# Split query and key logits in a second attention, with earlier bias loads, respread row products and two softmax groups moved to GpSimd

## The reference, cut to what matters

```python
# first model, attention layer
logits = einsum('bqhc,bqkc->bqhk', q_lat, c_sel) + bias      # bias = rel_bias[t5_bucket(dist)]
p = softmax(logits)                                          # keys chosen by a top-k of a score
# adaLN of the second model
shift, scale, gate = split(silu(cond) @ w_ada + b_ada, 3)    # two rows cond: c and c_ctx
# second model, attention ("second attention" below): 8 heads of 64
q = rms_norm(heads(z_q), q_norm_g) * 64 ** -0.5
k = rms_norm(heads(z_k), k_norm_g)                           # latent keys and context keys
s = concat([q . k_local + rpb bias (or -1e30), q . k_context])
out = softmax(s) @ [v, v_context]
```

## Time and profile before

| what | value |
|---|---|
| median of 3 runs | 860.97 us (860.26 to 863.52) |
| profiled execution | 861.54 us, its span 859.5 us |
| TensorE busy | 848.9 us (99% of the span), granted clock 1.0 throughout |
| VectorE, ScalarE, GpSimd busy | 698.2, 484.3, 130.0 us |
| memory traffic | 167.88 MB, mean 195 GB/s |

### The profile page before, as it was taken

One profiled execution on the slowest core, in us unless ns is written; L12 is line 12 of the kernel. 1 busy time (PEld: TensorE's weight loads), 2 busy tenths in 40 slices (PEclk: granted clock), 3 DMA queues, 4 the chain that ended last, 5 costly groups with the idle time before them and its releaser, 6 DMA issues.

```text
span 859.5 us, 18107 instructions
## 1 busy us (share of the span) xinstructions
PE 848.9 (99%) x7062; PEld 813.6 (95%) x7062; DVE 698.2 (81%) x1096; ACT 484.3 (56%) x710; POOL 130.0 (15%) x147
## 2 busy tenths in 40 slices
PE   8999999999999999999999999999999999999998
PEld 7999999999999997799999999989899898999998
DVE  5998798898888899786667666677758998998895
ACT  6796555555444466765555444363367557645742
POOL 3140000014322000000000222132203314012000
PEclk9999999999999999999999999999999999999999
DMA  8744667779999730246666666576445554455552
GB/s 318 299 149 147 221 229 245 244 258 294 296 289 267 216 128 20 93 162 214 196 195 196 203 193 195 167 214 220 149 148 172 171 161 159 148 174 177 207 180 98
DMA packets 48050, 167.88 MB, mean 195 GB/s; under 512 B 5969, under 2 KB 7393, under 8 KB 47729
## 3 DMA queue, kind: packets, MB, share of 16 engines
q1 hardware_dynamic: 41840, 146.82, 52.0%
q0 software_dynamic: 5856, 20.00, 8.0%
q10 hardware_dynamic: 288, 0.15, 0.1%
HBM read 165.50 MB, written 1.44 MB: 194 GB/s over the span
## 4 chain that ended last, share of the span: by engine, by line
PE 74%; DVE 14%; DMA 6%; ACT 3%; issue 2%; SPq 0%; POOL 0%; DVEq 0%; ACTq 0%
PE bank L546 22%; PE bank L550 22%; PE bank L551 22%; DMA raw<-weights 5%; DVE wlo L1416 4%; DVE xc L1498 1%; DVE ada_prod L1558 1%; PE bank L813 1%; ACT whi L1030 1%; PE bank L898 1%; PE bank L900 1%; PE bank L899 1%; PE bank L939 1%; PE bank L949 1%; DMA x<-x_in 1%
## 5 line engine op out<-in xcount | busy, mean ns | idle before, releaser
L1416 DVE TENSOR_TENSOR wlo<-raw,whi 128x1024 fp32r<-128x1024 f32 x266 | 326.8, 1262 | 86.1 <-ACT whi L1030 85.5
L550 PE MATMUL bank<-xl,whi 128*128 128x256 f32 x1328 | 369.7, 278 | 0.0
L546 PE MATMUL bank<-xh,whi 128*128 128x256 f32 x1310 | 367.5, 281 | 1.9 <-DVE xl L1438 1.7
L551 PE MATMUL bank<-xh,wlo 128*128 128x256 f32 x1328 | 368.4, 277 | 0.0
L1030 ACT ACTIVATE whi<-raw 128x1024 fp32r<-128x1024 f32 x266 | 272.3, 1054 | 152.6 <-PE bank L551 99.6
L546 PEld LDWEIGHTS bank<-xh,whi 128*128 128x128 f32 x1310 | 245.8, 188 | 10.9 <-issue 7.1
L550 PEld LDWEIGHTS bank<-xl,whi 128*128 128x128 f32 x1328 | 249.4, 188 | 0.3
L551 PEld LDWEIGHTS bank<-xh,wlo 128*128 128x128 f32 x1328 | 249.2, 188 | 0.0
L551 PE MATMUL bank<-hhi,wlo 128*128 128x256 f32 x560 | 155.1, 277 | 0.0
L546 PE MATMUL bank<-hhi,whi 128*128 128x256 f32 x554 | 154.1, 278 | 0.0
L550 PE MATMUL bank<-hlo,whi 128*128 128x256 f32 x512 | 142.2, 278 | 0.0
(11 more groups left out here) (311 smaller groups left out, 1032.1 us busy)
## 6 DMA issues: line engine op xcount, KB each, us to landing
raw<-weights SPq DMA_DIRECT2D x266, 512.0 KB, 4.3
ada_raw<-ada_w POOLq DMA_DIRECT2D x24, 512.0 KB, 5.7
plain<-plain_w SPq DMA_DIRECT2D x8, 512.0 KB, 8.5
relB<-rel_scratch POOLq DMA_DIRECT2D x8, 256.0 KB, 8.8
bl<-rpb_in POOLq DMA_DIRECT2D x32, 64.0 KB, 3.4
plain<-plain_w SPq DMA_DIRECT2D x4, 256.0 KB, 5.7
cond<-cond_in POOLq DMA_DIRECT2D x1, 1024.0 KB, 8.5
cx<-ctx_in POOLq DMA_DIRECT2D x1, 1024.0 KB, 8.5
```

What stands on the lines that cost most here:

```text
L546: mmul(dst, hi, rh, start=start, stop=False)
L550: mmul(dst, hi, rlo, start=False, stop=False)
L551: return mmul(dst, lo, rh, start=False, stop=stop)
L1416: V_.tensor_tensor(wlo[:, sl], raw[:, sl], whi[:, sl].bitcast(F32), ALU.subtract)\
```

## The change

The logits of the second attention are made from split operands: ACT copies `kk` and `q2` into `hch` and `xh[8..11]` (`qk_hi`), DVE subtracts into `hcl` and `xl[8..11]` (`qk_lo`), and `logits2` makes three fp32r products for each head instead of one float32 product. Tile 0 of this is placed ahead of the split of the first chunks of cg on both engines, tiles 1 to 3 after the first unit of cg. The eight `relB` loads are issued right after the table is stored. The order of the adaLN rows is new: two gate rows are summed beside rec_out, eight rows beside up0, and the other fourteen over the tiles of down0 as listed in `ADA_DOWN`. The pieces of the first two plain chunks hold half a chunk's row each (2 KB). For the groups 0 and 1 of the first attention GpSimd scales the probabilities.

```diff
@@ -93,9 +93,10 @@
-ADA_ORDER = [0, 1, 2, 3, 4, 5, 6, 7, 8, 16, 9, 17, 10, 18, 11, 19, 12, 20, 13, 21, 14, 22, 15, 23]
+ADA_ORDER = [16, 17, 0, 1, 2, 3, 4, 5, 6, 7, 8, 18, 9, 19, 10, 20, 11, 21, 12, 13, 22, 14, 23, 15]
 ADA_M = 3 * DT
-ADA_DOWN = 8
+ADA_UP = 2
+ADA_DOWN = ((10, 11), (12, 13), (14, 15), (16, 17), (18,), (19, 20), (21, 22), (23,))
@@ -340,8 +341,8 @@
-                part = slice(j * CH // 4, (j + 1) * CH // 4)
-                sp.dma_start(plain[:, 0:2, part], plain_w[0:2, :, part].rearrange("c p n -> p c n")).then_inc(s_head[j], 16)
+                part = slice(j % 2 * CH // 2, (j % 2 + 1) * CH // 2)
+                sp.dma_start(plain[:, j // 2, part], plain_w[j // 2][:, part]).then_inc(s_head[j], 16)
@@ -427,6 +428,17 @@
+            def load_rel_bias(m):
+
+                p0 = m * RCOPY
+                pool.dma_start(relB[p0:p0 + RCOPY], bass.AP(tensor=rel_scratch.tensor, offset=P - 1 - p0,
+                                                            ap=[[H1 * RLEN - 1, RCOPY], [RLEN, H1], [1, S]]))\
+                    .then_inc(S_["rel_bias_loaded"], 16)
+
+            pool.wait_ge(S_["rel_stored"], 16)
+            for m in range(DT):
+                load_rel_bias(m)
+
             for h in range(2):
@@ -437,17 +449,10 @@
+            load_ada(2)
+            load_ada(3)
             pool.wait_ge(S_["chunk_used"], 2 * U0["up0"])
             pool.dma_start(cx[:], ctx_in).then_inc(S_["ctx_loaded"], 16)
-            for i in range(2, ADA_DOWN + 2):
-                load_ada(i)
-
-            def load_rel_bias(m):
-
-                p0 = m * RCOPY
-                pool.dma_start(relB[p0:p0 + RCOPY], bass.AP(tensor=rel_scratch.tensor, offset=P - 1 - p0,
-                                                            ap=[[H1 * RLEN - 1, RCOPY], [RLEN, H1], [1, S]]))\
-                    .then_inc(S_["rel_bias_loaded"], 16)
@@ -461,13 +466,13 @@
                 add_ctx_squares(m)
-                for i in (ADA_DOWN + 2 * m + 2, ADA_DOWN + 2 * m + 3):
-                    if i < ADA_M:
-                        load_ada(i)
-
+                for i in ADA_DOWN[m + 1] if m < DT - 1 else ():
+                    load_ada(i)
+
+            for m in range(DT):
+                load_ada(4 + m)
             pool.dma_start(wiw[:], wi_in).then_inc(S_["wi_loaded"], 16)
-            pool.wait_ge(S_["rel_stored"], 16)
-            squares_by_tile(3, 0, ahead_of_tile, load_rel_bias)
+            squares_by_tile(3, 0, ahead_of_tile)
@@ -477,6 +482,12 @@
                 G.tensor_tensor(cx[:, m], cx[:, m], rctx[:], ALU.mult).then_inc(S_["ctx_scaled"], 1)
+            for g in range(2):
+                pool.wait_ge(S_["sums_inverted"], g + 1)
+                for i in range(4):
+                    sl = slice(i * P, (i + 1) * P)
+                    ins = G.tensor_scalar(pt[:, g % 3, sl], pt[:, g % 3, sl], rden[:, g % 2, i:i + 1], None, ALU.mult)
+                ins.then_inc(S_["probs_ready"], 1)
             squares_by_tile(5, 1, scale_ctx)
@@ -621,10 +632,11 @@
                             pe.wait_ge(S_["xg_ready"], k + 1)
-                            mm = mmul(bank[2 * c][:, 0:S], plain[:, c, k * P:(k + 1) * P], gate[:, k],
+                            w0 = (4 * (j % 2) + 2 * c + k % 2) * P
+                            mm = mmul(bank[2 * c][:, 0:S], plain[:, j // 2, w0:w0 + P], gate[:, k],
                                       start=k == 0, stop=k == DT - 1)
-                        if j == 3:
-                            mm.then_inc(S_["plain_used"], 1)
+                    if j % 2:
+                        mm.then_inc(S_["plain_used"], 1)
@@ -930,14 +942,18 @@
                 t, b = p // 2, p % 2
-                if p == 0:
-                    pe.wait_ge(S_["qk_normed"], 8)
-                else:
+                if b == 0:
+                    pe.wait_ge(S_["qk_lo"], t + 1)
+                if p:
                     pe.wait_ge(S_["logits2_read"], 2 * p)
-                for e in range(2):
-                    lo = 64 * e
-                    mmul(LOGIT[e][:, :], q2[lo:lo + 64, t, b * P:(b + 1) * P], kk[lo:lo + 64, t], start=True, stop=True)\
-                        .then_inc(S_["logits2_full"], 1)
+                tok = slice(b * P, (b + 1) * P)
+                for n, (q, k) in enumerate(((xh, hch), (xh, hcl), (xl, hch))):
+                    for e in range(2):
+                        rows = slice(64 * e, 64 * e + 64)
+                        mm = mmul(LOGIT[e][:, :], q[rows, 8 + t, tok], k[rows, 2 * t:2 * t + 2].rearrange("p a n -> p (a n)"),
+                                  start=n == 0, stop=n == 2)
+                        if n == 2:
+                            mm.then_inc(S_["logits2_full"], 1)
@@ -1350,11 +1366,20 @@
             dsts = {"cg": (cg, ACT.Sigmoid), "za": (za, ACT.Silu), "cz": (cz, ACT.Silu), "bz": (bz, ACT.Silu)}
+            def qk_hi(t):
+                act.wait_ge(S_["qk_normed"], t + 1)
+                A(hch[:, 2 * t:2 * t + 2], two(kk[:, t]), ACT.Copy).then_inc(S_["qk_hi"], 1)
+                act.wait_ge(S_["qk_normed"], BT + t + 1)
+                A(xh[:, 8 + t], q2[:, t], ACT.Copy).then_inc(S_["qk_hi"], 1)
+            qk_hi(0)
             ahead(U0["ca"] + 1)
...
                     ahead(U0[name] + i)
+                    if name == "cg" and i == 0:
+                        for t in range(1, BT):
+                            qk_hi(t)
                     if name in dsts:
@@ -1553,7 +1578,7 @@
                         ch.wait()
-                    else:
+                    elif used is not None:
                         dve.wait_ge(S_["ada_used"], used)
@@ -1565,7 +1590,7 @@
                 dve.wait_ge(s_adaw[i % 2], 16 * (i // 2 + 1))
-                ada_sums(i % 2, i, lambda c: ada[:, t, c:c + 1], 1 if t >= 2 * DT else 2)
+                ada_sums(i % 2, i if i else None, lambda c: ada[:, t, c:c + 1], 1 if t >= 2 * DT else 2)
@@ -1620,19 +1645,18 @@
-                i0, c = (-5, -5, -4, -4)[r], r % 2
-                n = 2 * i0
+                i0, c = (-3, -3, -2, -2)[r], r % 2
+                n = 2 * (i0 - ADA_UP)
                 if c == 0:
                     dve.wait_ge(s_adaw[i0 % 2], q * 16 + 16 * (i0 // 2 + 1))
-                    if not (isinstance(q, int) and q * 2 + i0 == 0):
-                        dve.wait_ge(S_["ada_used"], q * 2 + i0)
+                    dve.wait_ge(S_["ada_used"], q * 2 + i0)
                 else:
...
                     dve.wait_ge(S_["ada_summed"], q * 4 + (n + 2))
-                    V_.tensor_copy(ada[:, bass.ds(q * 2 + i0, 1), :], ada_pair[:].unsqueeze(1))\
+                    V_.tensor_copy(ada[:, bass.ds(q * 2 + (i0 - ADA_UP), 1), :], ada_pair[:].unsqueeze(1))\
                         .then_inc(S_["ada_used"], 1)
@@ -1642,6 +1666,8 @@
                 add_pair(0, j)
+                if j in (1, 2):
+                    ada_tile(j - 1)
@@ -1681,8 +1707,8 @@
                     if name == "0":
-                        ada_tile(ADA_DOWN + 2 * m)
-                        ada_tile(ADA_DOWN + 2 * m + 1)
+                        for i in ADA_DOWN[m]:
+                            ada_tile(i)
                     if name == "1":
@@ -1807,7 +1833,13 @@
                 dve.wait_ge(S_["exp_ready"], g + 1)
-                ch.link(V_.reciprocal(rden[:, g % 2, 0:2 * nt], den[:, g % 2, 0:2 * nt]))
+                ins = V_.reciprocal(rden[:, g % 2, 0:2 * nt], den[:, g % 2, 0:2 * nt])
+                if g < 2:
+                    ins.then_inc(S_["sums_inverted"], 1)
+                    return
+                ch.link(ins)
+                if g == 2:
+                    dve.wait_ge(S_["probs_ready"], 2)
                 for i in range(2 * nt):
@@ -1968,7 +2000,13 @@
+            def qk_lo(t):
+                dve.wait_ge(S_["qk_hi"], 2 * t + 2)
+                V_.tensor_tensor(xl[:, 8 + t], q2[:, t], xh[:, 8 + t].bitcast(F32), ALU.subtract)
+                V_.tensor_tensor(hcl[:, 2 * t:2 * t + 2], two(kk[:, t]), hch[:, 2 * t:2 * t + 2].bitcast(F32), ALU.subtract)\
+                    .then_inc(S_["qk_lo"], 1)
             ahead(U0["ca"] + 1)
+            qk_lo(0)
             copy_out("ca", 1, ca[:, 2:4])
@@ -1987,6 +2025,9 @@
                     attend(u)
+                    if name == "cg" and i == 0:
+                        for t in range(1, BT):
+                            qk_lo(t)
                     if name == "za" and i == 0:
@@ -2185,7 +2226,9 @@
         return np.ascontiguousarray(units.reshape(-1, P, 2, CH).transpose(0, 2, 1, 3).reshape(-1, P, CH))
-    return chunks(STAGES), chunks(PLAIN)
+    plain = chunks(PLAIN)
+    plain[0:2] = plain[0:2].reshape(2, P, 2, 2, CH // 4).transpose(2, 1, 3, 0, 4).reshape(2, P, CH)
+    return chunks(STAGES), plain
```

(2 more changed lines are left out.)

2 lines of the change are left out of this document (1 added, 1 removed).

## The result

The changed kernel takes 866.35 us at the median of eight runs (864.91 to 867.39), the kernel before 861.78 beside it: a ratio of 1.0051, 95% interval 1.0036 to 1.0066. It is slower by 0.5%, where 854.7 us and at most 859.2 had been forecast. The profiled execution took 866.25 us with a span of 864.4, against 859.5 before.

The account below looks back on a forecast made before the run. TensorE was taken as the bound from 14 us to the end; -0.2 (longer rows) - 4.0 (down0) - 0.8 (GpSimd) - 1.4 (logits) + 0.1 (stall) = -6.3 gave 854.7 us. Range 851.9 to 859.2; the forecast's own 852.3 to 856.5.

Parts of the forecast that it names:

- Bias loads early: Bias loads issued at 35.7 to 40.5 us, before GpSimd's next product at 41.24; cost 0, up to 1 us.
- rival 6: Early bias loads only crowd the start and delay GpSimd; +1 and pieces of down0's 4.0 lost, 857 us; chance 0.03.
- What down0 gains: In down0, fewer bytes make weights just in time: 1.7 us wait goes, quick pace holds; gain 4.0 us, bounds 1.5 and 4.7.
- Two groups by GpSimd: First attention: GpSimd scaling two groups lets the last bank of queries start earlier; gain 0.8 us.
- rival 2: GpSimd's scalings slow or in VectorE's way: +0.9 instead of -0.8, 856.4 us; chance 0.1.
- Logits of the second attention: Three fp32r products a head, heads side by side: 0.89 us a pair instead of 1.06; gain 1.4 us over eight.
- rivals 4 and 5: Logits' products run one after another, 860.3 us (chance 0.05); or each also waits for its weights, 863.6 us (chance 0.04).
- Rival 3: Changed timing leaves units beside the second attention at the slower pace; eight lost cost 1.8 us, 856.5 us; chance 0.1.
- Longer rows: First two plain chunks in half as many descriptors bring the last piece of `x` forward; gain 0.2 us, bound 0 to 1.4.

Follow-up runs that it names:

- e12: The kernel before with one change: bias loads stay in down0, but each piece writes every eighth partition instead of sixteen neighbours; 857.99 us, ratio 0.9953.
- e9: The kernel before with the second attention's logits from split queries and keys alone; 860.36 us, ratio 0.9988.
- e5: The changed kernel with bias loads moved to about 62 us, behind GpSimd's last product of the recurrence, pieces into every eighth partition; 856.04 us, ratio 0.9933.
- e8: The changed kernel with one bias load behind each adaLN row beside up0, pieces into every eighth partition; 855.97 us, ratio 0.9931.
- e13: The changed kernel with bias loads back in down0, pieces into every eighth partition; 856.15 us, ratio 0.9933.
- e3: The changed kernel, bias loads still early, each piece into every eighth partition instead of sixteen neighbours; 860.00 us, ratio 0.9984.
- e15: The changed kernel, bias loads still early, each piece into every second of 32 partitions; 861.51 us, ratio 0.9999.
- e16: The changed kernel, bias loads still early, as sixteen pieces of eight partitions, every fourth of 32; 857.24 us, ratio 0.9960.
- e17: The changed kernel, bias loads still early, as sixteen pieces of eight partitions, every sixteenth of 128; 860.15 us, ratio 0.9992.
- e6: The changed kernel with bias loads moved to about 62 us, pieces still into sixteen neighbouring partitions; 861.50 us, ratio 1.0001.

## Why the prediction was wrong

It failed at one step, "Bias loads early": "The 2 MB move out of down0 into a stretch where splits wait for VectorE, not for memory. Cost 0, up to 1." It cost 10.5 us: the wait of 9.0 us and 1.7 us at the lower clock, less the 0.3 that the start had won. What was worked out was when GpSimd could issue the loads, and that came true. What was left out was how fast a piece lands, and what lands beside it. The row was there to be read, in the view by tile of the kernel before:

```profile
L448 POOL DMA_DIRECT2D relB<-rel_scratch x8: 584/606/606, 198.1 to 277.6; - x8
...
DMA to landing us min/median/max: 5.2/8.8/9.4
```

That is 8.8 us for 256 KB. The weight chunks beside them in the same stretch, of 512 KB each, took 7.5 us at the median:

```profile
L339 SPq DMA_DIRECT2D raw<-weights x28: 332/333/333, 197.7 to 279.8; - x28
...
DMA to landing us min/median/max: 3.5/7.5/10.0
```

Those issued between 36 and 60 us, where the loads were to go, took 4.8. And the two chunks issued at 38 and 39 us in the kernel before were split 3 us after their landing, so 3 us of delay was all that stretch could take. Behind them ScalarE had the whole second half of the recurrence. The mechanism was named in rival 6, "the bias loads only move the crowd to the start", but its price was put at 1 us plus pieces of the 4.0, its chance at 0.03.

*What down0 gains.* Size right (4.0 forecast, 4.1 measured, or 3.0 against the kernel before's quickest profiled down0; the pace and the wait as described), cause wrong in one half. The forecast held that 313 GB/s were wanted and 279 to 300 could be delivered. But that ceiling was made by the pieces' shape: e12 keeps all the bytes, delivers 297 GB/s at a share of 0.89, and wins the whole term. The 2 MB did not have to leave. That the size came out was in part luck.

*Two groups by GpSimd.* 0.9 us by the sums (the wait fell from 1.4 to 0.4), 0.8 forecast. A scaling takes 0.59 us, not 0.5, which hurt nothing. Here is VectorE in the kernel after, without and with GpSimd at work (332.25 to 334.60 us):

```profile
327.86 0.41 DVE L1788 MATCH_REPLACE8 score<-m,score 128x256 f32<-128x256 f32 x1
...
332.57 0.41 DVE L1788 MATCH_REPLACE8 score<-m,score 128x256 f32<-128x256 f32 x1
```
```profile
332.25 2.35 POOL L489 TENSOR_SCALAR pt<-pt,rden 128x128 f32<-128x128 f32 x4 [40.12 <-DVE rden L1836]
```

The same 0.41 us: VectorE did not slow, and rival 2 is out. The rule of the Trainium skill ("SBUF — State Buffer", "Who interferes with whom") that the forecast weighed agrees with these rows.

*Logits of the second attention.* Timeline of TensorE in the kernel after, first pair:

```profile
632.32 0.50 PE L953 MATMUL bank<-hch,xh 64*128 64x512 f32 x2
632.66 0.40 PE L953 MATMUL bank<-hcl,xh 64*128 64x512 f32 x2
632.90 0.40 PE L953 MATMUL bank<-hch,xl 64*128 64x512 f32 x2
633.22 0.39 PE L557 MATMUL bank<-xh,whi 128*128 128x256 f32 x1
```

The heads run side by side (two products a row), 0.90 us from the first start to the next unit instead of 1.06, no stall ahead: 1.3 us over eight pairs, 1.4 forecast; rivals 4 and 5 are out. Only 0.6 of it reached the end. Rival 3 took the rest, at one place: the units behind the first two pairs run at the slow pace now, 95 products in 11 us where the kernel before had 98. The first starts of the first three pairs are 12.41 and 13.28 us apart instead of 12.14 and 13.23; from there on the distance is 14.45 instead of 14.62, the full gain. e9 has the same distances, so this comes with the split logits alone.

```profile
633.50:644.50 11.00, 11.00 (x95) 11.00 (x95) 6.82 (x13) 9.04 (x15) 0.00 (x0) 1.00 0.39 133
```
```profile
628.00:639.00 11.00, 11.00 (x98) 10.95 (x96) 4.05 (x7) 6.62 (x10) 0.00 (x0) 1.00 0.35 123
```

*Longer rows*: the first sum of squares starts at 13.68 us instead of 13.97, 0.3 for 0.2.

So of the terms that bring time four were about right in size, the logits but for what the pace took back. e5, e8 and e13, the change with its bias pieces spread and kept out of the start, take 855.97 to 856.15 us; they beat both kernels, the one before by 0.67 to 0.69%. The span of e5's profiled execution is 5.7 us shorter than before's, 0.6 short of the 6.3 forecast, about what the pace took back.

Two slips in the forecast's arithmetic changed nothing. Its own range of 852.3 to 856.5 isn't the sum of the three bounds named beside it, which give 851.9 to 857.5; and with 216 ns a product the gain of the logits is 1.7 us, not 1.8.

## What to carry to other kernels

Before a transfer is moved to an idle stretch, read three things there: how long it takes to land and how many bytes that is (is it slow for its size?), how much time the transfers beside it have to spare, and what lies behind their wait in the program of the engine that waits. A DMA share near 1 at 163 GB/s, where 288 were reached with other rows, was the sign of slow transfers here, not of many bytes; look at where the rows of a piece land before moving it. Where an engine's program puts late data ahead of work that doesn't need it, a few us of delay become the delay of everything behind.

## What the hardware showed that was not expected

**Where a transfer's rows land set the rate, and others beside it lost by it.** With equal bytes and source, in 40 to 60 us: eight pieces into sixteen neighbours each 163 GB/s of total traffic at a full share, into every eighth partition 288, into every second of 32 281; sixteen pieces of eight, into every fourth 292, into every sixteenth 185. The Trainium skill ("SBUF — State Buffer", "Door 1: The DMA port swizzle (why `[64,N]` ≈ `[32,N]`)") gives the rule that orders these: four neighbours share one of 16 ports, and so do the four that lie 32 above them in the same half of 64; the other half has ports of its own. By it sixteen neighbours reach 4 ports, both e3's and e15's pieces 8, e16's 8 and e17's 4, and the runs agree in that order. That these ports are the cause was tested through this order alone, and it orders the rates, not the delays of the weights (e15 and e17 above).

**The clock after a stop.** In the kernel after, the granted clock fell while TensorE stood in its wait of 9.0 us and was 0.50 in 67 to 77 us. In e3 a wait of 2.2 us at the same place left it at 0.86 in 60 to 72 us, with 16 products at the lower level, which is why up0 began 3.6 us late and not 2.2. In e6 a wait of 2.8 us, from 98.7 to 101.5 us, left it at 1.00 in 101 to 112 us. In e12 it was 0.58 in 330 to 334 us, among the short products of the first attention that follow the wait of 1.4 us for queries; the kernel before has the same wait and products at 1.00:

```profile
330.00:334.00 4.00, 4.00 (x26) 2.47 (x22) 2.78 (x18) 2.76 (x11) 0.00 (x0) 0.58 0.00 0
```

The same kernel goes both ways: of e3's twelve executions five kept a mean clock of 1.000 and took 858.29 to 859.30 us, the other seven had 0.995 to 0.998 and took 859.72 to 862.56. Only one of the twelve was profiled, so the waits of the others are not known; but a median of such a kernel depends on how many of its executions lost the clock. What decides was not tried.
